# Weight chunks of four rows by 256 columns in place of two by 512 in the two up products

## What is computed

```python
D_MODEL, D_FF, SEQ = 2048, 5632, 256
# first block
hf = rmsnorm(x, norm_ffn_w)
u = causal_dwconv(hf @ w_up, conv_w, conv_b)        # w_up: 2048 x 11264
a, b = jnp.split(u, 2, axis=-1)
x = x + (jax.nn.silu(a) * b) @ w_down               # w_down: 5632 x 2048
# second block
up = h @ w_up_2                                     # 2048 x 11264
up = causal_depthwise_conv(up, conv_w_2) + conv_b_2
gate, val = jnp.split(up, 2, axis=-1)
f = (jax.nn.silu(gate) * val) @ w_down_2
```

## Time and profile before

| | us |
|---|---|
| median of 3 runs | 2672.49 |
| the profiled execution | 2673.49 |
| its span | 2671.3 |
| TensorE matmuls busy | 2645.7 |
| VectorE busy | 1788.4 |
| ScalarE busy | 1335.7 |

### The profile page before, as it was taken

The page is one execution under the profiler, slowest core; times in us unless marked ns, Lnnn a source line. Parts: engine busy times, 40 slices in busy tenths (PEclk is TensorE's granted clock), DMA queues, the critical chain, the costliest instruction groups (busy, mean ns, idle before and its releaser), DMA issues.

```text
span 2671.3 us, 42031 instructions
## 1 busy us (share of the span) xinstructions
PE 2645.7 (99%) x15857; PEld 2342.3 (88%) x15857; DVE 1788.4 (67%) x2165; ACT 1335.7 (50%) x1625; POOL 158.2 (6%) x111
## 2 busy tenths in 40 slices
PE   8999999999999999999999999999999999999998
PEld 8888898889999988888888889998788888888887
DVE  6777557656544677777775456898777777776444
ACT  4554364464533655555553344444665555554443
POOL 4000300000100200000001222000020000000000
PEclk9999999999999999999999999999999999999999
DMA  7655456556544566665556665655555666666664
GB/s 245 190 165 182 142 161 193 171 162 190 182 134 157 180 192 189 188 188 188 188 188 190 190 190 175 196 186 174 169 184 189 188 188 189 188 188 206 191 192 146
DMA packets 249952, 487.12 MB, mean 182 GB/s; under 512 B 15021, under 2 KB 68293, under 8 KB 249312
## 3 DMA queue, kind: packets, MB, share of 16 engines
q1 hardware_dynamic: 248352, 476.12, 56.8%
q0 software_dynamic: 1472, 9.19, 1.0%
HBM read 483.12 MB, written 2.13 MB: 182 GB/s over the span
## 4 chain that ended last, share of the span: by engine, by line
PE 93%; DVE 5%; ACT 1%; issue 1%; DMA 0%; SPq 0%; DVEq 0%; ACTq 0%
PE ps L1986 92%; DVE w_lo L1260 2%; DVE acc L1767 1%; DVE op L1333 1%; DMA raw<-in_weights 0%; ACT w_hi L764 0%; DVE x_res L1928 0%; DVE ya L1831 0%; SPq L582 0%; DVE ua L1294 0%; ACT lnz L1168 0%; DVE y_lo L1325 0%; PE ps L2285 0%; DVE ya L1833 0%; DVE r_j L1591 0%
## 5 line engine op out<-in xcount | busy, mean ns | idle before, releaser
L1986 PE MATMUL ps<-op,w_hi 128*128 128x512 f32 (+1 forms) x6400 | 1653.2, 349 | 13.9 <-DVE op L1333 12.6
L1260 DVE TENSOR_TENSOR w_lo<-raw,w_hi 128x1024 fp32r<-128x1024 f32 x900 | 1123.5, 1251 | 809.7 <-ACT w_hi L764 808.6
L764 ACT ACTIVATE w_hi<-raw 128x1024 fp32r<-128x1024 f32 x900 | 951.7, 1061 | 1123.3 <-PE ps L1986 1092.4
L1986 PE MATMUL ps<-op,w_lo 128*128 128x256 f32 x5024 | 1108.1, 280 | 0.0
L1986 PEld LDWEIGHTS ps<-op,w_lo 128*128 128x128 f32 x5024 | 951.5, 189 | 162.4
L1986 PEld LDWEIGHTS ps<-op,w_hi 128*128 128x128 f32 x6400 | 989.0, 191 | 19.1 <-issue 16.0
L1986 PE MATMUL ps<-g,w_hi 128*128 128x512 f32 x704 | 219.6, 393 | 0.0
L1986 PE MATMUL ps<-w_hi,g 128*128 128x512 f32 x704 | 217.7, 390 | 0.0
L1986 PE MATMUL ps<-w_hi,op 128*128 128x512 f32 x512 | 163.4, 393 | 0.0
L1986 PEld LDWEIGHTS ps<-w_hi,g 128*128 128x128 f32 x704 | 132.1, 188 | 30.2
L1986 PEld LDWEIGHTS ps<-g,w_lo 128*128 128x128 f32 x704 | 132.4, 188 | 30.0
(11 more groups left out here) (289 smaller groups left out, 1511.5 us busy)
## 6 DMA issues: line engine op xcount, KB each, us to landing
raw<-in_weights SPq DMA_DIRECT2D x900, 512.0 KB, 4.5
x_res<-in_x SPq DMA_DIRECT2D x8, 256.0 KB, 8.3
mem_x<-in_mem POOLq DMA_DIRECT2D x1, 2048.0 KB, 8.5
x_res<-in_x POOLq DMA_DIRECT2D x1, 2048.0 KB, 10.7
w_row<-row_dram POOLq DMA_DIRECT2D x2, 1024.0 KB, 8.1
out_x<-x_res SPq DMA_DIRECT2D x3, 512.0 KB, 2.9
rel_rev<-rel_dram POOLq DMA_DIRECT2D x1, 1024.0 KB, 6.2
hg_con<-in_hg_consts POOLq DMA_DIRECT2D x1, 576.0 KB, 7.4
```

The costliest lines, as they stand in the source:

```text
L764: nc.scalar.activation(w_hi[:, s], raw[:, s], ACT.Copy).then_inc(hi_rounded, 1)
L1260: TT(w_lo[:, s], raw[:, s], w_hi[:, s].bitcast(F32), ALU.subtract).then_inc(chunk_split, 1)
L1986: return nc.tensor.matmul(out, lhsT, rhs, start=start, stop=stop, skip_group_check=True)
```

## The change

In blocks 2 to 21 of up and of up_2 a chunk is four weight rows of 256 columns. Chunks 0 to 3 of a block bring rows 0 to 15 of its tiles 0 and 1, chunks 4 to 7 those of its tiles 2 and 3. TensorE does such a chunk as tile by tile four long matmuls (four rows k), then their four short ones. Bytes, the number of chunks and of matmuls, and all waits between the engines stay as they are. Blocks 0 and 1 keep the old chunks. SyncE's loop over up is split in two: one pass of the old form, ten of the new.

```diff
+            def narrow_blocks(g):
+                with sp.Fori(1, g.blocks // 2) as i:
+                    for h in range(2):
+                        for c in range(g.chunks):
+                            n = g.chunks * h + c
+                            s = n % SLOTS
+                            at = 2 * h + c // 4
+                            four = columns[:, bass.ds(g.first_chunk + 2 * g.chunks * i + 4 * (c % 4), 4)]
+                            sp.wait_ge(chunk_split, g.first_chunk + 2 * g.chunks * i + (n - (SLOTS - 1)))
+                            sp.dma_start(raw[:, s].rearrange("p (c w) -> p c w", c=4), four[:, :, at * TOK:(at + 1) * TOK]).then_inc(raw_loaded[s], 16)
-            half_blocks(GM["up"])
+            half_blocks(GM["up"], 1)
+            narrow_blocks(GM["up"])
...
-            half_blocks(GM["up_2"])
+            half_blocks(GM["up_2"], 1)
+            narrow_blocks(GM["up_2"])
...
+            FOUR_ROWS = [(kind, r, t) for t in range(2) for kind in (HI, LO) for r in range(4)]
-            def product_halves(g, both, ready, at=None, peeled=2, sequence=TWO_TILES):
+            def product_halves(g, both, ready, at=None, peeled=2, sequence=TWO_TILES, narrow=False):
...
-                        for kind, row, t in sequence:
-                            k = 2 * c + row
-                            cs = slice((4 * row + t) * P, (4 * row + t + 1) * P)
+                        by_four = narrow and not (static and b < 2)
+                        for kind, row, t in FOUR_ROWS if by_four else sequence:
+                            k = 4 * (c % 4) + row if by_four else 2 * c + row
+                            cs = slice((2 * row + t) * P, (2 * row + t + 1) * P) if by_four else slice((4 * row + t) * P, (4 * row + t + 1) * P)
+                            t = 2 * (c // 4) + t if by_four else t
...
-            product_halves(GM["up"], op, halves("up"), beside_up(GM["up"], 3), 4, TWO_TILES)
+            product_halves(GM["up"], op, halves("up"), beside_up(GM["up"], 3), 4, TWO_TILES, True)
```

More of the change, by code:

```diff
@@ L593, in _, with half_blocks @@
             columns = A["weights"].rearrange("c p w -> p c w")
-            def half_blocks(g):
-                with sp.Fori(0, g.blocks // 2) as i:
+            def narrow_blocks(g):
[8 more added lines that the diff above has]
+                            sp.dma_start(raw[:, s].rearrange("p (c w) -> p c w", c=4), four[:, :, at * TOK:(at + 1) * TOK]).then_inc(raw_loaded[s], 16)
+            def half_blocks(g, pairs=None):
+                with sp.Fori(0, g.blocks // 2 if pairs is None else pairs) as i:
                     for h in range(2):
@@ L2523, in beside_up_2 @@
                 return at
-            product_halves(GM["up_2"], op, halves("up_2"), beside_up_2(), 4, TWO_TILES)
+            product_halves(GM["up_2"], op, halves("up_2"), beside_up_2(), 4, TWO_TILES, True)
             product_tokens(GM["down_2"], g_hi, g_lo, DOWN_2_CHUNKS, lambda pair: READY["down_2"] + 2 * pair + 2)
```

## The result

The changed kernel takes 2679.68 us (median of 10 runs, 2677.94 to 2681.03) against 2672.84 us for the kernel before (10 runs, 2671.70 to 2674.88). The ratio is 1.0025, with a 95% interval of 1.0017 to 1.0033: slower by 6.8 us, about the smallest step that a measurement of this kernel can tell. The prediction said 2670.6 us and gave slower by over 0.2% a chance of 0.18. The time lies inside its range, on the side that was not forecast.

What follows compares the result with a forecast made beforehand. TensorE's matmul pace, start to start, was taken to bound up and up_2. Halving the excess saves 2.9 ns on each of 640 eights, 1.9 us, all else nothing: 2672.5 - 1.9 = 2670.6 us, range 2665.5 to 2682.5.

Steps and rivals of the forecast that it cites:

- What bounds the kernel: In up and up_2 only TensorE's distance from one matmul's start to the next sets the time; matmuls busy 99% of span.
- the price of the new eight: Four longs plus four shorts in up and up_2: 2.9 ns under today's two groups' 1.3930 us, 1.9 us in all.
- the excess: What up's group of two longs and two shorts takes above runs of one length and down: 5.8 ns an eight.
- The ends I had put around it: Saving in up and up_2: 0 if the excess goes by the matmul, 4.4 us if all goes, as in down.
- The sign I had reasoned to: Faster in up and up_2: half the excess goes, as it appears where lengths mix and op is read; 1.9 us.
- Rival 1: Shorts in runs of four wait for their weights, 0.1201 us, longs unchanged: +9.8 us, 2682.3 us; chance 0.15.
- The formula under its "Back-to-back issue gap": TensorE's matmuls cost columns / 2.4 + 2.5 ns whatever the order, 2600 ns a chunk; the change would do nothing.
- a fixed price of 0.0133 us a matmul: TensorE: each matmul averages 0.0133 us over its columns in down and pure runs; held against rivals of changed pace.
- Rivals 3: Four longs in a row onto one bank cost 0.2291 us each, as in out_2: +2.4 us, 2674.9 us; chance 0.08.
- 4: Smaller DMA pieces land late and TensorE waits, one chunk in 20 by 2 us: +32 us, 2704 us; chance 0.03.
- Rival 2: Longs inside runs of four in up and up_2 fall to 0.2267 us, shorts stay: -12.7 us, 2659.8 us; chance 0.06.
- Rival 5: TensorE's pace does not depend on the order of lengths: no change, 2672.5 us; chance 0.15, inside the forecast's 0.68.

Runs made afterwards that it cites:

- experiment 9: Kernel before with down's chunks in runs of four, two rows of two tiles long, then short: 2673.28 us beside 2673.25.
- Experiments 4: Kernel before with tile op 64 bytes further in each partition and all behind op 128 bytes further: 2662.07 us beside 2673.47.
- 10: Kernel before with op 96 bytes further and everything behind it 288 bytes further: 2704.72 us beside 2673.25.
- experiment 2: Kernel before, old chunks, in order four longs onto four different banks, then their four shorts: 2679.64 us beside 2673.47.
- experiment 8: Kernel before, old chunks, one long and one short in turn, run twice: 2677.85 us beside 2670.51, then 2680.51 beside 2673.25.

## Why the prediction was wrong, point by point

**What bounds the kernel: right.** TensorE's pace set the time before and after, and 6.4 of the 6.8 us lie in the two products.

**The term that failed: the price of the new eight.** The step was "I take that the excess shows once for each pass through long and short, so that half of it goes", -2.9 ns an eight, -1.9 us. Measured: +9.9 ns an eight, 1.403 against 1.393 us. Over the pace of runs of one length, a pass costs 3.4 ns with runs of two and 16 with runs of four, so halving the passes did not halve what they cost. The step took one reading, of one run length at one distance, for a price per pass. The ends I had put around it, 0 and 4.4 us, came from down and from runs of one length; neither bounds it, since both are cases in which the excess is absent. down at its own distance has no surcharge at two or at four (experiment 9), so it could say nothing about op's.

**The sign I had reasoned to.** "The excess appears where lengths are mixed and op is read and is absent in both pure runs" was not quite true, and the word that mattered was op. The run of shorts alone reads op as well and has no excess, so at this distance the mix is needed; but at 64 bytes the same mix goes below 0.0133 us a matmul. The excess belongs to the mix at op's distance, and I priced the mix alone.

**Rival 1, shorts in a run of four at 0.1201 us with the longs unchanged, +9.8 us: nearest.** Its 0.475 us for four shorts was measured as 0.47 to 0.48, its 0.933 for four longs as 0.93, and its condition, longs above 0.2295 us, was met with 0.2325. It was worth +9.8 us and came to +6.4: the shorts cost 13.4 ns an eight of the 15.3 it gave them, and the longs gave back 3.4 where it gave none. Its mechanism, that each short waits for its own weights, is not shown as I put it: at g's distance four shorts after four longs take 0.115 us each. The page TensorE: Matmul & The Clock Gate of the Trainium skill, whose section "LDWEIGHTS (loading the stationary operand)" I had weighed for it, gives 107 ns a load. The records of loads in the kernel before last longer, and beside shorts they overlap, since shorts start 0.115 us apart with a load each:

```profile
L1986 PEld LDWEIGHTS ps<-op,w_lo x288: 187/188/188, 1199.8 to 1299.9; 128*128 128x128 f32 x144
```

So they neither confirm nor exclude 107 ns, and that figure does not tell why the same run of shorts takes 0.47 to 0.48 us at one distance and 0.46 at another. The formula under its "Back-to-back issue gap", columns / 2.4 + 2.5 ns, is given there for the isolated gap of a single matmul; I had used it for this stream, where it does not hold: the 2.600 us a chunk that I estimated from it stand against 2.760 to 2.827 from the same sixteen matmuls.

**Against rival 1 I had set a fixed price of 0.0133 us a matmul, only booked differently between neighbours.** It was the argument that kept its chance at 0.15. Experiments 4 and 10 gave 0.690 and 0.7066 us a group, 0.0125 and 0.0167 us a matmul over the columns. There is no such fixed price: all three kinds of stage that had it changed when the distance did, down to 0.690 us a group, shorts alone to 0.118 us and longs alone to 0.234.

**Rivals 3 and 4: out.** Four longs onto one bank cost what four onto four banks cost (experiment 2). The new DMAs landed in 3.5 us, sooner than the old.

**Rival 2** fell with the longs, which stayed at 0.2325 us where it needed 0.228. **Rival 5**, no change at all, fell with the 20 ns a chunk.

**What stays open.** Why runs of four cost more than runs of two at a distance of 0 (20 ns a chunk), less so at 64 (7 ns) and not at 192 (down) is described by these runs, not explained. That distance modulo 256 bytes between the two operands in SBUF matters would fit a reading of weights and of the moving stream that get in each other's way, but that is a guess: no run here isolates it. The two paces of experiment 8 say that the distance and the order are not all, since both were the same in both.

## What to carry to other kernels

Where TensorE is busy throughout, cost an edit by its pace, start to start, and do not expect reordering of equal work to be free or its price to scale with the number of changes: try the run lengths, they are not in order (2.787, 2.806 and 2.793 us for two, four and eight). Before the order, try the place: 64 bytes ahead of one tile, with what follows it kept in place modulo 256, were worth 16 us, more than twice what this change of order lost, and a stage in which the same tile changes its role from moving to stationary can pay for it, so read every stage afterwards. And where two executions of one program differ, look in the trace for a stretch at the low clock before you look for a cause in the program.

## What the runs showed of the hardware that I had not expected

- The distance between moving and stationary operand in the partition, modulo 256 bytes, moves a chunk of eight long and eight short float32r matmuls between 2.760 us (64 bytes) and 2.827 (96 bytes), in runs of two, at a granted clock of 1.00 and with nothing waited for. Moving both together by 64 bytes changes nothing (2.787).
- The same sequence of single long and short matmuls ran at 2.827 us a chunk in the first blocks of up, at 2.773 in the rest of up and at 2.827 in up_2, in two runs alike; within up the pace changed at two other matmuls between them.
- In runs of eight the last matmuls go at the pace of a stream of one length (0.2267 and 0.120 us), and the 20 ns that a pass costs lie in the first ones.
- DMAs of four 1 KB pieces a partition landed after 3.5 us in the median in up, those of two 2 KB pieces after 4.7.
